# State space input products: one-pass fp32r over four stacked high/low pieces, fetched through DRAM scratch, in a two-block fp32 model kernel

## The reference, cut to what matters

```
h = rms_norm(x, norm_mix_g) * (1 + sc1) + sh1
u, q, k, v, ga, gb = split(h @ w_in)            # u: 1024 wide
bu_re = einsum('blgp,gnp->blgn', u32, bbar_re)  # 64 groups, 16 inputs -> 64 states each
bu_im = einsum('blgp,gnp->blgn', u32, bbar_im)
s = associative_scan(complex a, bu)             # along the 256 tokens
y_ssm = glu(gelu(C_re s_re - C_im s_im + d * u))
merged = sigmoid(ga) * (y_ssm @ w_proj_ssm) + sigmoid(gb) * (y_att @ w_proj_attn)
x = x + g1 * (merged @ w_out)
```

## Time and profile before

| | |
|---|---|
| median of 3 runs | 2926.87 us |
| profiled execution | 2925.44 us |
| its span | 2923.7 us |
| PE busy | 2863.5 us, 98% |
| DVE busy | 2158.6 us, 74% |
| ACT busy | 1482.9 us, 51% |
| DMA queue of SP (q1) | 601.92 MB, 59.1% of 16 engines' span |
| stage (first to last input product) | 1585.8 to 1914.3 us |

### The profile page before, as it was taken

How to read it: one execution, slowest core, us unless ns; L and a number is a source line. 1 busy time by engine, 2 the same in 40 slices (tenths; PEclk the granted TensorE clock), 3 DMA queues, 4 the chain that set the end, 5 groups by cost and what they waited for, 6 DMA issues and landing times.

```text
span 2923.7 us, 50756 instructions
## 1 busy us (share of the span) xinstructions
PE 2863.5 (98%) x17162; PEld 2503.3 (86%) x17162; DVE 2158.6 (74%) x3172; ACT 1482.9 (51%) x2124; POOL 453.1 (15%) x188
## 2 busy tenths in 40 slices
PE   7999999999999999999999999999999999999998
PEld 6888888888888888888897778788898888888887
DVE  6777777777688988888878899876786436465466
ACT  4454444444354444444445777765545444444443
POOL 0111101111000000000000000000004445455443
PEclk9999999999999999999999999999999999999999
DMA  6544444555568888878775445466685566767655
GB/s 236 169 156 144 158 158 158 165 163 173 176 212 302 317 304 308 305 283 335 283 280 184 166 166 173 166 203 230 233 315 179 187 206 245 241 222 249 205 182 180
DMA packets 199095, 637.03 MB, mean 218 GB/s; under 512 B 32312, under 2 KB 46776, under 8 KB 198208
## 3 DMA queue, kind: packets, MB, share of 16 engines
q1 hardware_dynamic: 165024, 601.92, 59.1%
q10 hardware_dynamic: 33952, 33.52, 3.6%
HBM read 619.61 MB, written 15.75 MB: 217 GB/s over the span
## 4 chain that ended last, share of the span: by engine, by line
PE 66%; issue 25%; DVE 5%; ACT 3%; DMA 1%; ACTq 0%; DVEq 0%; POOL 0%; SPq 0%; POOLq 0%
PE gemm L590 40%; PE gemm L594 21%; DVE wl L1616 2%; ACT wh L1056 1%; PE gemm L587 1%; PE gemm L588 1%; DVE dT L1814 1%; DVE dW L1812 1%; DVE gB L1834 0%; ACT gA L1157 0%; DVE cb L1621 0%; ACT gB L1150 0%; PE side L725 0%; PE side L752 0%; PE side L757 0%
## 5 line engine op out<-in xcount | busy, mean ns | idle before, releaser
L590 PE MATMUL gemm<-xs,wh 128*128 128x512 f32 x5088 | 1610.2, 398 | 16.5 <-DVE stage L1621 8.1
L1056 ACT ACTIVATE wh<-raw 128x1024 fp32r<-128x1024 f32 x939 | 983.2, 1058 | 963.1 <-PE gemm L594 848.5
L1616 DVE TENSOR_TENSOR wl<-raw,wh 128x1024 fp32r<-128x1024 f32 x811 | 1033.0, 1279 | 427.2 <-ACT wh L1056 403.5
L594 PEld LDWEIGHTS gemm<-xs,wl 128*128 128x128 f32 x5088 | 956.9, 188 | 213.3
L594 PE MATMUL gemm<-xs,wl 128*128 128x256 f32 x5088 | 1006.1, 279 | 0.0
L590 PEld LDWEIGHTS gemm<-xs,wh 128*128 128x128 f32 x5088 | 774.1, 188 | 44.9 <-issue 29.2
L590 PE MATMUL gemm<-hid,wh 128*128 128x512 f32 x2112 | 666.0, 396 | 8.4 <-DVE xacc L1636 2.3
L594 PEld LDWEIGHTS gemm<-hid,wl 128*128 128x128 f32 x2368 | 436.5, 188 | 90.7
L594 PE MATMUL gemm<-hid,wl 128*128 128x256 f32 x2368 | 467.6, 279 | 0.0
L1544 POOL TENSOR_TENSOR wl<-raw,wh 128x1024 fp32r<-128x1024 f32 x128 | 348.7, 2729 | 361.7 <-ACT wh L1056 360.4
L590 PEld LDWEIGHTS gemm<-hid,wh 128*128 128x128 f32 x2112 | 319.1, 188 | 11.8 <-ACT wh L1056 3.2
(11 more groups left out here) (406 smaller groups left out, 1960.4 us busy)
## 6 DMA issues: line engine op xcount, KB each, us to landing
raw<-in_stream SPq DMA_DIRECT2D x940, 512.0 KB, 3.9
ada_a<-in_ada SPq DMA_DIRECT2D x144, 512.0 KB, 5.1
ada_b<-in_ada SPq DMA_DIRECT2D x48, 512.0 KB, 4.8
stash<-stage ACTq DMA_DIRECT2D x12, 512.0 KB, 3.3
att<-stash ACTq DMA_DIRECT2D x8, 384.0 KB, 4.3
x<-in_x SPq DMA_DIRECT2D x4, 512.0 KB, 5.6
A_scratch<-gB ACTq DMA_DIRECT2D x8, 256.0 KB, 3.6
Em<-E_scratch ACTq DMA_DIRECT2D x8, 256.0 KB, 5.9
```

Source lines behind the costliest of these rows:

```text
L590: mm(G[n][:, :], w, moving, start=first, stop=False, skip_group_check=True)
L594: op = mm(G[n][:, 0:T] if whole else G[n][:, T:2 * T], wl[:, slot, at:at + P], rhs(sl * SLAB_K + k)[:, 0:T], start=False, stop=last, skip_ ...
L1056: A(wh[:, slot, :], raw[:, slot, :], ACT.Copy).then_inc(hi_ready, 1)
L1616: tt(wl[:, slot, :], raw[:, slot, :], wh[:, slot, :].bitcast(F32), ALU.subtract).then_inc(lo_ready[slot], 1)
```

## The change

For chunks 1 to 7 the input products are no longer fp32. ACT makes high parts of the chunk's inputs u and of its transposed coefficients (`high_parts`), DVE the two low parts, all in a tile `parts`. SP writes the four combinations (high·high, low·low, high·low, low·high) to a DRAM scratch in 4 DMAs (`parts_away`) and reads them back with the four pieces of each group of 16 rows stacked along 64 partitions (`stacked`: 8 DMAs for the slots of pairs 0 to 2, 8 more for pair 3). A product is then four fp32r matmuls of 64 rows and 256 columns, in two row halves. Chunk 0 stays as it was. The masking of `lbt` remains for chunk 0 alone and goes to ACT; the transpose moves from o=15 to o=7. The final1 scalings leave the stage for slots 11 to 35 of the attention hook. The fourth `crs` of a chunk moves from o=21 to o=22. In attention group n=6 ACT copies all banks before its slot work; in the merge groups the high and low parts are made in slot 0 of the next group, and ACT's prefetch moves from slot 0 to slot 2.

```diff
+    pairs4 = nc.alloc_sbuf_tensor_at("pairs4", [P, 4, 2 * T], F32R, offset=hid_at)
+    u_parts = nc.alloc_sbuf_tensor_at("parts", [P, 4, T], F32R, offset=...)
+    X_AT = (11, 11, 12, 13, 13, 15, 17, 19, 19, 20, 21, 21, 23, 33, 33, 35)
...
+        def parts_away(j):
+            sp.wait_ge(S("u_low"), j)
+            wait(sp, three_in, LOADED + 128 * (j - 1) if j > 1 else 0)
+            wait(sp, fourth_in, LOADED + 128 * (j - 1) if j > 1 else 0)
+            for piece, (first, step) in enumerate(((0, 2), (1, 2), (0, 3), (1, 1))):
+                sp.dma_start(parts_dram[piece].rearrange("p (v t) -> p v t", v=2),
+                             u_parts[:, first:first + step + 1:step, :].bitcast(F32)).then_inc(parts_out, 16)
+        def stacked(j, lo, hi, landed, e):
+            if e == 0:
+                sp.wait_ge(parts_out, LOADED + 64 * j)
+                sp.wait_ge(S("mp_bu"), QK_HEADS + 4 * (j - 1) + hi)
+            for piece in range(4):
+                rows = parts_dram[piece, 64 * e:64 * e + 64, :].rearrange("(i r) w -> r i w", r=16)
+                sp.dma_start(pairs4[64 * e + 16 * piece:64 * e + 16 * piece + 16, lo:hi, :].bitcast(F32),
+                             rows[:, lo:hi, :]).then_inc(landed, 16)
+        for j in range(1, SSM_CHUNKS):
+            for sl in range(3 * RING):
+                slab(Q_MIX + 3 * j + sl // RING, sl % RING)
+                if sl == 1:
+                    parts_away(j)
+                elif sl in (3, 4):
+                    stacked(j, 0, 3, three_in, sl - 3)
+                elif sl in (5, 6):
+                    stacked(j, 3, 4, fourth_in, sl - 5)
...
 (PE, ssm)
+                elif j > 0 and i == 0:
+                    pe.wait_ge(three_in, LOADED + 128 * j)
+                elif j > 0 and i == 3:
+                    pe.wait_ge(fourth_in, LOADED + 128 * j)
...
+                            both = pairs4[64 * e:64 * e + 64, 2 * (i % 2) + i // 2, :]
+                            op = mm(bu[:, e, w, :], both[:, T + w * P:T + (w + 1) * P], both[:, 0:T], start=True, stop=True)
-            elif o == 15 and j + 1 < SSM_CHUNKS:
+            elif o == 7 and j + 1 < SSM_CHUNKS:
                 states(j + 1)
 (ACT)
+        def high_parts(j):
+            act.wait_ge(S("mp_bt"), QK_HEADS + j + 1)
+            act.wait_ge(bank_freed, 4 * (G_U + 1 + j // 4))
+            wait(act, parts_out, LOADED + 64 * (j - 1) if j > 1 else 0)
+            A(u_parts[:, 0, :], uT[:, j, :], ACT.Copy)
+            A(u_parts[:, 2, :], ps0[:, 0:2 * P], ACT.Copy).then_inc(S("u_high"), 1)
...
+            elif o == 8 and j + 1 < SSM_CHUNKS:
+                high_parts(j + 1)
 (DVE)
-            elif o % 6 == 3:
+            elif o == 11 and j + 1 < SSM_CHUNKS:
+                dve.wait_ge(S("u_high"), j + 1)
+                low(u_parts[:, 1, :], uT[:, j + 1, :], u_parts[:, 0, :])
+                low(u_parts[:, 3, :], ps0[:, 0:2 * P], u_parts[:, 2, :]).then_inc(S("u_low"), 1)
+            elif o in (3, 9, 15, 22):
...
-            elif o in (10, 16):
-                link(stt(x[:, k, :], x[:, k, :], V("final1", k, 1), xbc[:, :], ALU.mult, ALU.mult))
-            if o == 17 and j + 1 < SSM_CHUNKS:
-                states(j + 1)
...
```

More of the change, by code:

```diff
@@ L275, in program @@
     top[0] += 2 * 4 * (8 * 144 - 4 * 64) - 4 * T
-    lbt = [nc.alloc_sbuf_tensor_at(f"lbt{n}", [P, 2, 2, P], F32, offset=at)
-           for n, at in enumerate((hid_at, hid_at + 4 * (2 * 8 * P + 2 * 4 * 64 + T)))]
+    pairs4 = nc.alloc_sbuf_tensor_at("pairs4", [P, 4, 2 * T], F32R, offset=hid_at)
+    u_parts = nc.alloc_sbuf_tensor_at("parts", [P, 4, T], F32R, offset=hid_at + 4 * (2 * 8 * P + 2 * 4 * 64 + T))
+    lbt = nc.alloc_sbuf_tensor_at("lbt", [P, 2, 2, P], F32, offset=hid_at + 4 * (2 * 8 * P + 2 * 4 * 64 + 5 * T))
     stage = place("stage", [P, 4, T])
@@ L346, in program @@
                                            "att0", "att1", "att2", "merge0", "merge1")}
+    parts_out, three_in, fourth_in = loads["x1"], loads["x2"], loads["x3"]
+    LOADED = 16
     norm_sq, norm_acc, norm_sum, norm_var, norm_rn, norm_bc = (
@@ L889, in states @@
             pe.wait_ge(S("m_bs"), QK_HEADS + j + 1)
-            wait(pe, S("m_lb"), QK_HEADS + j)
+            wait(pe, S("m_lb"), QK_HEADS + 1 if j == 1 else 0)
+            wait(pe, S("u_low"), j - 1)
             for w in range(2):
@@ L1316, in states, with masked @@
             A(bs[:, 1, :], bb2[:, j * P:(j + 1) * P], ACT.Copy).then_inc(S("m_bs"), 1)
+        def masked():
+            act.wait_ge(S("mp_bt"), QK_HEADS + 1)
+            both = ps0[:, 0:2 * P].rearrange("p (w i) -> p w i", w=2)
+            for a in range(2):
+                op = A(lbt[:, :, a, :], both, ACT.Copy, scale=L("emask")[:, a:a + 1])
+            op.then_inc(S("m_lb"), 1)
+        def high_parts(j):
[4 more added lines that the diff above has]
+            A(u_parts[:, 2, :], ps0[:, 0:2 * P], ACT.Copy).then_inc(S("u_high"), 1)
         def outputs(j):
@@ L1358, in before_ssm @@
                 states(0)
+            elif slot == 30:
+                masked()
         restart()
@@ L1386, in ssm @@
                 tables(pair + 1)
-            if o == 13 and j + 1 < SSM_CHUNKS:
+            if o == 5 and j + 1 < SSM_CHUNKS:
                 states(j + 1)
+            elif o == 8 and j + 1 < SSM_CHUNKS:
+                high_parts(j + 1)
             if j > 0:
@@ L1480, in _, with merged @@
                 A(sgA[:, :, :], sgA[:, :, :], ACT.Tanh, scale=0.5).then_inc(S("p_t"), 1)
+        def merged(i):
+            act.wait_ge(S("mrg"), i + 1)
+            A(hid2[:, 16 + 4 * i:20 + 4 * i, 0:T], smm[i % 2][:, :, :], ACT.Copy, scale=0.5).then_inc(S("mrg_hi"), 1)
         def merge(i):
             def hook(slot):
-                if slot == 0 and i < 3:
+                if slot == 0 and i > 0:
+                    merged(i - 1)
+                elif slot == 1:
+                    if i == 0:
+                        keep_late(7)
+                    act.wait_ge(loads[f"merge{i % 2}"], 32 * (i // 2 + 1))
+                    A(sgm[i % 2][:, :, :], sgm[i % 2][:, :, :], ACT.Tanh, scale=0.5).then_inc(S("mg_t"), 1)
+                elif slot == 2 and i < 3:
                     act.wait_ge(loads["stash"], 16 * min(15 + i, 16))
@@ L1490, in hook @@
                     fetch_merge(i + 1)
-                elif slot == 1:
-                    if i == 0:
-                        keep_late(7)
-                    act.wait_ge(loads[f"merge{i % 2}"], 32 * (i // 2 + 1))
-                    A(sgm[i % 2][:, :, :], sgm[i % 2][:, :, :], ACT.Tanh, scale=0.5).then_inc(S("mg_t"), 1)
             return hook
@@ L1500, in _ @@
                  tail_at=EVAC_ACT)
-            act.wait_ge(S("mrg"), i + 1)
-            A(hid2[:, 16 + 4 * i:20 + 4 * i, 0:T], smm[i % 2][:, :, :], ACT.Copy, scale=0.5).then_inc(S("mrg_hi"), 1)
+        merged(3)
         for i in range(4):
@@ L2200, in before_ssm @@
                                       (ps1, ps0)[n % 2][:, :].rearrange("p (a i) -> p a i", a=2)).then_inc(S("t_set"), 1)
-            elif slot == 30:
-                states(0)
         restart()
@@ L2296, in moba @@
                 gated(ATT_SLOT.index(slot - 1) - 1)
+            for k in [k for k in range(KC) if X_AT[k] == slot]:
+                link(stt(x[:, k, :], x[:, k, :], V("final1", k, 1), xbc[:, :], ALU.mult, ALU.mult))
             if slot not in MOBA_AT:
@@ L2331, in _, with merged @@
                 gated(n)
+        def merged(i):
+            dve.wait_ge(S("mrg"), i + 1)
+            dve.wait_ge(S("mrg_hi"), i + 1)
+            o = hid2[:, 16 + 4 * i:20 + 4 * i, :]
+            stt(o[:, :, T:2 * T], smm[i % 2][:, :, :], 0.5, o[:, :, 0:T].bitcast(F32), ALU.mult, ALU.subtract
+                ).then_inc(S("mrg_lo"), 1)
         for i in range(4):
@@ L2337, in out, with hook @@
                     add(G_MRG + i, c, mt[:, c, :], 2)
-            walk(Q_MRG + i, 4, split, pool=POOL_NONE, tail=out, tail_at=EVAC_DVE)
+            def hook(slot):
+                if slot == 0 and i > 0:
+                    merged(i - 1)
+            walk(Q_MRG + i, 4, split, hook, pool=POOL_NONE, tail=out, tail_at=EVAC_DVE)
             added(G_MRG + i)
```

34 lines of the change are left out of this document (14 added, 20 removed).

## The result

The changed kernel takes **2933.53 us** (median of 8 runs, 2931.37 to 2940.06), the kernel before 2926.85 (8 runs beside it, 2922.03 to 2929.46). The ratio is 1.0028, 95% interval 1.0018 to 1.0039: 6.7 us more in the medians, where 2915 was forecast and 2903 to 2929 was the range. The prediction was wrong in the sign. The profiled execution took 2932.84 us, its span is 2931.1.

The account below looks back on a forecast made before the run. PE was taken to bound the stage, DVE 5 us per round behind. Terms -11.2 - 1.3 - 2.0 + 1.0 + 2.0 = -11.5 us from 2925.44 gave 2913.9, as a median 2915 us; own range 2907 to 2922, with rivals 2903 to 2929.

Parts of the forecast that it names:

- The pieces through DRAM: SP's writes and reads of the stacked pieces: on time or up to 3 us late; priced at nothing, +10 us in range.
- a wait of PE of 1 or 2 us only takes the place of the stall at the next adds: PE in the stage while DVE is the limit: the reason late pieces were given no cost.
- Rival (2): Pieces late at each of seven chunks' first product: 2943 at 5 us each, loss beyond 2.6 us per chunk; chance 0.13.
- The price from the page: The skill's DMA rule, 2.0 us fixed plus bytes at 436 GB/s: four 96 KB reads in 2.9 us, in time.
- The products on PE: Input products in the stage: 0.50 us each instead of 1.15, 28 of them, saving 18.2 us of PE work.
- DVE's amount: DVE's work in the stage: net -7.2 us, -1.8 per round, so busy 75.25 us per round.
- DVE's order: DVE's work by group within a round: A 3.45 us worse against PE, B 0.8 worse, C 0.8 better.
- 2.0 us of a new stall at A and left 2.27 at C: PE stalls per round at ends of groups A and C, waiting for DVE's adds: A's new, C's unchanged.
- -11.2 was forecast: The stage's term: per round -5.2 + 2.0 = -3.2 us, over 3.5 rounds -11.2 us (-6 to -19).
- Behind the stage: After the stage: n=6 copies -1.3 us, merge groups -2.0, x scalings in attention +1.0.
- ACT: ACT's two extra copies per chunk, 5.3 us, and chunk 0's mask: hidden in its 40.7 us waiting for PE; nothing.
- The clock: PE's matmuls at the lower clock level after some four more stalls: +2 us (0 to +6).

Follow-up runs that it names:

- e1_once: The changed kernel, but only chunk 1's pieces go through DRAM and chunks 2 to 7 reuse them: 2907.57 us, ratio 0.9937.
- e2_early: The changed kernel with transpose, high and low parts, writes and first eight reads of the pieces moved three to five slots sooner: 2908.94 us, ratio 0.9942.
- e8_reads: The changed kernel with one edit, SP's first eight reads of a chunk one weight slab sooner: 2906.65 us, ratio 0.9941.
- e3_relief: The kernel before with the edits behind the stage, `crs` behind the adds and x scalings in attention; fp32 products stay: 2913.08 us, ratio 0.9954.
- e4_behind: The kernel before with only the edits behind the stage (n=6 copies, merge halves later): 2920.35 us, ratio 0.9984.
- e9_products: e2_early with `crs` and the scalings of x put back in their old places: 2920.63 us, ratio 0.9985.
- b1_slots: e8_reads with the scalings of x moved away from attention slots ahead of a softmax step: 2905.64 us, ratio 0.9932.

## Why the prediction was wrong, step by step

**The step that failed is "The pieces through DRAM ... I take nothing for it".** It had two parts. The first was the path. Where the issue would stand was nearly right: I had the last of the eight reads begin 4.3 us ahead of the old product, less 1 to 3 for PE's sooner coming, and it begins 3.4 us ahead (1711.4 to 1714.8). The landing was not: I took 4.4 us from eight loads of 128 KB that stood in ACT's queue with no weight load between them, and the reads land after 6.0 in the median (5.5 for the 96 KB reads that a chunk's first product needs, 6.4 for the 32 KB ones of pair 3) and after 7.3 at the place shown. They are sixteen to a chunk in groups of four, between 512 KB loads in one queue, which themselves land after 4.0 us instead of 3.3. What part of this is the company and what part the shape (16 partitions) no run tells apart: in e1_once, where only chunk 1's pieces move, its sixteen reads take 6.1 us in the median too. So the pieces came 2.9 us late on average, up to 3.9, at each of the seven chunks, where "on time or up to 3 us late" at every second one had been the forecast.

The second part was the belief that "a wait of PE of 1 or 2 us only takes the place of the stall at the next adds". At 2.9 us it replaced little: within the stage the stalls on `stage` are 4.2 us here, 6.5 in e1_once and 10.3 in e2_early, so of the 20.3 us 2.3 to 6.1 were absorbed. Rival (2) had counted 7. What I had not counted is the matmuls behind each wait at the lower clock, 7.8 us of busy time in the stage. With them rival (2)'s break-even is not 2.6 us but (11.5 + 7 - 7.8) / 7 = 1.5. By the same sum 2.9 us would be a loss of 9.6; measured are 6.7. e1_once, e2_early and e8_reads show the cause in three ways: no DMAs behind chunk 1, all DMAs early, and the reads alone one slab early give 2907.57, 2908.94 and 2906.65.

The Trainium skill (DMA: Bandwidth & Descriptors, on the anatomy of one DMA) would put four reads of 96 KB at an estimated 2.9 us; its figures are a fit to DMAs that GpSimd issues, which the prediction left out, and these stand in SP's queue. The measurement decides: 6.0 in the median in the changed kernel, 4.9 in e8_reads. The price from the page was the further off of my two.

**The products on PE: right.** 0.52 us where 0.50 was forecast; 17.6 us of work by these steps where 18.2 was forecast. PE's busy time over the whole stage falls by 15.3 us (316.7 in e3_relief, 301.4 in e8_reads, both at a granted clock of 1.00).

**DVE's amount: right; DVE's order: less bad than forecast.** Busy 75.42 us per round (forecast 75.25), and in e8_reads, with the pieces nearly on time, the round is 79.9 us (81), with PE at 77.5 (76.8) and DVE at 94% of the round (93% or more). I had 2.0 us of a new stall at A and left 2.27 at C, 15 us in all. e1_once has 0.7 and 1.5, 6.5 us in the stage; e8_reads has 4.7 us of them there and 4.1 at the DMA. C's stall is 1.4 in the changed kernel, so its adds did come sooner with `crs` gone from ahead of them. The stage is 17.5 us shorter than before in e8_reads and 14.9 in e2_early, where -11.2 was forecast. With the pieces on time the kernel would have been just under my own range's lower end of 2907.

**Where the gain is from: partly not where I put it.** I counted the saving from PE's work and let DVE give part of it back. The runs in a row tell it otherwise: the edits behind the stage 4.7 us (e4_behind by its ratio), `crs` behind the adds 6.1, the scalings 2.6 or nothing (ratios 0.9963 and 0.9954, medians 2912.74 and 2913.08), and the fp32r products with their pieces, from e3_relief to e8_reads, 3.8 by the ratios (a difference that their intervals do not keep clear of nothing) and 6.4 by the medians, 7.9 in the stage. That 7.9 is 15.3 us of PE's busy time less 7.5 of idle time that is new, 4.1 of it for the DMA and 3.0 for DVE's adds. The products without the new order bring nothing (e4_behind and e9_products). Of 17.6 us taken from PE, less than half reaches the end.

**Behind the stage: right, as far as 2 us of scatter let one say.** -5.0 us for the two edits (forecast -3.3); the scalings add nothing or 1.1 (1005.0 in e4_behind and in e3_relief, 1006.1 in e8_reads; forecast +1.0). In the changed kernel it is -1.7 for all of them (forecast -2.3). The stall of 2.2 us at `fxg` is 0.8 now, and the two at `mt` are gone from the list of waits. PE's waits for the softmax steps are 1.0 us before and 5.1 after; 2.4 of these stand in e4_behind, which has no scaling in attention, and in b1_slots other slots for the scalings did not remove them, so that a single scaling is the cause is not shown.

**ACT: right.** Its two copies per chunk cost nothing that a wait shows; it waits 52.7 us for PE.

**The clock: the size was wrong.** I added 2 us for all stalls, from the one in the earlier trace rows; behind the other two stalls of 2.27 us in the kernel before, the pair takes 0.70 and 0.75 us. In the changed kernel it costs 3.0 us of PE busy time in one round and 7.8 in the stage. In e8_reads, where no wait in the stage is over 1.6 us, the granted clock of the round is 1.00.

## What to carry to other kernels

Data that goes through DRAM between two engines is priced from the last issue of its last DMA, with the landing time of small DMAs in company, and from the engine that waits, not from an average of the queue: here 3 us of lateness in each of seven places turned a gain of 18 us into a loss of 7, and one slab's place in the queue turned it back. Where a second engine is at 91%, first put its own work behind what frees the banks (6.1 us here for one line), and only then take work from the bound engine. Leave a hand-over that PE waits for a margin of its own: a wait costs its length, and behind six of the seven here came slower matmuls as well.
